# A chunked RWKV inverse kept in PSUM with two pairs in flight, and the one-token sample's state update moved into the feed-forward stage

## The reference, cut to what matters

```python
def step(S, inp):
    r_t, w_t, k_t, v_t, kk_t, b_t = inp
    Sa = jnp.einsum('bhij,bhj->bhi', S, -kk_t)
    S = S * w_t[:, :, None, :] + Sa[..., None] * b_t[:, :, None, :] + v_t[..., None] * k_t[:, :, None, :]
    return S, jnp.einsum('bhij,bhj->bhi', S, r_t)
```

## Time and profile before

| | before |
|---|---|
| median of three runs | 1666.39 us |
| the profiled execution, its span | 1667.1 us |
| TensorE busy | 1566.2 us, 94% of the span |
| VectorE busy | 1140.1 us, 68% |
| ScalarE busy | 858.5 us, 51% |
| GpSimd busy | 262.7 us, 16% |
| layer 0, from the first level product to the last `solve` | 133.46 us (449.41 to 582.87) |
| layer 1, the same stretch | 135.50 us (1268.40 to 1403.90) |

### The profile page before, as it was taken

One profiled execution on the slowest core, in us unless ns is written; L12 is line 12 of the kernel. 1 busy time (PEld: TensorE's weight loads), 2 busy tenths in 40 slices (PEclk: granted clock), 3 DMA queues, 4 the chain that ended last, 5 costly groups with the idle time before them and its releaser, 6 DMA issues. The chain is left out here.

```text
span 1667.1 us, 41414 instructions
## 1 busy us (share of the span) xinstructions
PE 1566.2 (94%) x17379; PEld 1486.8 (89%) x17379; DVE 1140.1 (68%) x1822; ACT 858.5 (51%) x1515; POOL 262.7 (16%) x259
## 2 busy tenths in 40 slices
PE   7999999989799899999999999999997989899997
PEld 6999999987688789999999999989775878799997
DVE  6565587795798667665575656968768886676654
ACT  5444464667444555444354444657673445554443
POOL 0000003001356431000000000030014554300000
PEclk9999999999899999999999999999998999999999
DMA  7555556471244545555454655644703463455552
GB/s 230 178 172 170 168 159 199 130 208 53 59 125 120 144 157 161 194 179 186 143 186 160 194 183 175 189 141 128 215 1 102 126 178 98 131 189 187 183 178 71
DMA packets 280650, 256.28 MB, mean 154 GB/s; under 512 B 48054, under 2 KB 268700, under 8 KB 280450
## 3 DMA queue, kind: packets, MB, share of 16 engines
q1 hardware_dynamic: 276698, 252.05, 48.5%
q10 hardware_dynamic: 3768, 1.59, 0.4%
HBM read 242.22 MB, written 11.38 MB: 152 GB/s over the span
## 5 line engine op out<-in xcount | busy, mean ns | idle before, releaser
L209 ACT ACTIVATE front_hi<-front_raw 128x1024 fp32r<-128x1024 f32 (+2 forms) x230 | 238.5, 1039 | 262.0 <-PE ps L234 255.5
L216 DVE TENSOR_TENSOR front_lo<-front_raw,front_hi 128x1024 fp32r<-128x1024 f32 (+1 forms) x210 | 252.2, 1201 | 109.0 <-ACT front_hi L209 108.2
L209 ACT ACTIVATE out_hi<-out_raw 128x1024 fp32r<-128x1024 f32 (+1 forms) x168 | 173.3, 1038 | 219.1 <-PE ps L234 205.1
L216 DVE TENSOR_TENSOR out_lo<-out_raw,out_hi 128x1024 fp32r<-128x1024 f32 (+1 forms) x148 | 183.9, 1243 | 108.1 <-ACT out_hi L209 107.3
L232 PE MATMUL ps<-front_h_hi,front_hi 128*128 128x264 f32 (+1 forms) x816 | 241.3, 296 | 4.9 <-DVE front_lo L216 3.3
L234 PE MATMUL ps<-front_h_hi,front_lo 128*128 128x264 f32 (+1 forms) x816 | 233.0, 286 | 0.0
L233 PE MATMUL ps<-front_h_lo,front_hi 128*128 128x264 f32 (+1 forms) x816 | 232.7, 285 | 0.0
L232 PE MATMUL ps<-ffn_h_hi,out_hi 128*128 128x264 f32 x704 | 200.7, 285 | 0.1
L233 PE MATMUL ps<-ffn_h_lo,out_hi 128*128 128x264 f32 x704 | 200.0, 284 | 0.0
L234 PE MATMUL ps<-ffn_h_hi,out_lo 128*128 128x264 f32 x704 | 199.8, 284 | 0.0
L232 PE MATMUL ps<-in_h_hi,front_hi 128*128 128x264 f32 x688 | 197.4, 287 | 0.0
(11 more groups left out here) (400 smaller groups left out, 3891.7 us busy)
## 6 DMA issues: line engine op xcount, KB each, us to landing
front_raw<-in_w_in SPq DMA_DIRECT2D x50, 1024.0 KB, 5.2
out_raw<-in_ffn_w_in SPq DMA_DIRECT2D x44, 1024.0 KB, 5.2
front_raw<-in_ffn_w_in SPq DMA_DIRECT2D x40, 1024.0 KB, 5.3
back_sample_rows<-row_scratch SPq DMA_DIRECT2D x160, 128.0 KB, 3.0
out_raw<-in_w_out SPq DMA_DIRECT2D x16, 1024.0 KB, 6.3
front_raw<-in_ffn_w_out SPq DMA_DIRECT2D x16, 896.0 KB, 4.6
out_raw<-in_ffn_w_out SPq DMA_DIRECT2D x16, 896.0 KB, 4.6
front_raw<-in_ffn_w_out SPq DMA_DIRECT2D x8, 1024.0 KB, 5.0
```

Of the source, the lines that this page charges most:

```text
L209: act.activation(self.hi[n % self.RING][:, 0:k, 0:w], self._raw(n), ACT.Copy).then_inc(self.hi_ready, 1)
L216: eng.tensor_tensor(self.lo[n % self.RING][:, 0:k, 0:w], self._raw(n), self.hi[n % self.RING][:, 0:k, 0:w].bitcast(F32), ALU.subtract).the ...
```

## The change

The inverse is made in another way:

- The sum of `x` stays in PSUM: `turn_x` starts it in a bank of its own (`XB + p % 2`), and `level_u` adds its product to it. ACT copies the sum to SBUF after each level (`x_copy(p, i)`).
- The transposed inverse is no longer made by a second product of each level, but by DVE from the copy, as a transposition of 32x32 blocks (`turn_blocks`). Only the last level keeps the product in the transposed form (`finish`).
- Two pairs are in flight: in a round TensorE does levels 2, 3, 4 of pair `g-1` and levels 0, 1 of pair `g`, by turns. `turn_x` of pair `g` stands near the start of its round, `gram` of pair `g+1` near its end, and `mask(g+1)` on DVE behind it.
- In the rounds, a sample pair now has only one product on DVE (old state with two rows, 128x1024) and one sum. The read-out is put together from those sums and from dot products of the vectors (`rec_products`, `rec_sums`, `sample_outputs`). Two rows are loaded, not five.
- The new state is made in the second feed-forward block (`SampleUpdate`): the state and three rows are loaded again, POOL multiplies two rows by a vector, DVE does three operations for each of 8 pairs, at m = 2, 4, 7, 9, 12, 14, 17 and 19 of the 22 steps, and SP stores. These transfers stand in SP's queue between the loads of weight pieces.
- On ACT, `norm3.act_root` moves behind the wait for two stores.

```diff
+class SampleUpdate:
...
+    def sp(self, sp, n):
+        if n == 0:
+            sp.wait_ge(*self.free)
+        if n >= 2:
+            sp.wait_ge(self.done, 3 * (n - 1))
+            sp.dma_start(self.new[n - 2], self.state[(n - 2) % 3][:]).then_inc(self.stored[(n - 2) % 3], 16)
+        if n < RT:
+            for h in range(2):
+                sp.dma_start(self.rows[h * HS:(h + 1) * HS, n % 2].rearrange("p v b j -> p v (b j)"),
...
+            sp.dma_start(self.state[n % 3][:], self.old[n]).then_inc(self.state_in[n % 3], 16)
...
+    def pool(self, pool):
+        for q in range(RT):
+            pool.wait_ge(self.rows_in[q % 2], 32 * (q // 2 + 1))
+            for i, x0 in ((1, self.env.sample_sums[:, q, 0]), (2, self.env.sample_v[:, q])):
+                row = self.rows[:, q % 2, i]
+                pool.tensor_tensor(row, row, x0.unsqueeze(2).to_broadcast([P, NS, HS]), ALU.mult).then_inc(self.products, 1)
...
+    def place(n):
+        return 2 + 5 * n // 2
+
+    def dve(self, dve, m):
...
+        for i, op in ((0, ALU.mult), (1, ALU.add), (2, ALU.add)):
...
+            dve.tensor_tensor(st0[:], st0[:], self.rows[:, q % 2, i], op).then_inc(self.done, 1)
```

```diff
                 for p in range(3, len(pieces)):
                     ws.load(sp, p)
+                    for n in range(RT + 2):
+                        if p == update.place(n) + 10:
+                            update.sp(sp, n)
...
+                def x_copy(p, i):
+                    if i:
+                        act.wait_ge(s("u_ps"), order_of[p, i - 1] + 1)
+                    else:
+                        act.wait_ge(s("x_ps"), p + 1)
+                    act.activation(x[:, p % 2].rearrange("p q t -> p (q t)"), ps[:, XB + p % 2, 0:4 * C], ACT.Copy).then_inc(s("x_in"), 1)
...
+                def turn_blocks(p, i):
+                    flat = lambda a: a.rearrange("p q t -> p (q t)")
+                    dve.wait_ge(s("x_in"), copied[p, i])
+                    dve.transpose(flat(xt[:, p % 3]), flat(x[:, p % 2])).then_inc(s("xt_in"), 1)
...
+                def sample_products(m):
...
+                    dve.tensor_tensor(prod[:], state[:, m % 2].unsqueeze(1).to_broadcast([P, 2, NS, HS]), rows[:, m % 2],
+                                      ALU.mult).then_inc(s("sampled"), 1)
+
+                def sample_sums(m):
+                    dve.wait_ge(s("sampled"), m + 1)
+                    dve.tensor_reduce(sums[:, m], prod[:], AX.X, ALU.add).then_inc(s("summed"), 1)
...
                 def level_u(p, i):
-                    n = LV * p + i
+                    n = order_of[p, i]
                     pe.wait_ge(s("t1_in"), n + 1)
-                    if n:
-                        pe.wait_ge(s("xt_up"), n)
-                    if i < LV - 1:
-                        blocks(UB, xt[:, p % 3], t1[:]).then_inc(s("u_ps"), 1)
-                    blocks(UB + 1, t1[:], xt[:, p % 3]).then_inc(s("ut_ps"), 1)
+                    if i:
+                        pe.wait_ge(s("xt_in"), turned_blocks(p, i))
+                    if i < LV - 1:
+                        blocks(XB + p % 2, 0, xt[:, p % 3], t1[:, n % 2], False, i == LV - 2).then_inc(s("u_ps"), 1)
+                    else:
+                        blocks(XB + p % 2, 4 * C, t1[:, n % 2], xt[:, p % 3]).then_inc(s("u_ps"), 1)
...
                 def solve(p):
 
-                    pe.wait_ge(s("xt_up"), LV * (p + 1))
+                    pe.wait_ge(s("xt_up"), p + 1)
```

More of the change, by code:

```diff
@@ L333, in act_hi @@
     def act_hi(self, act, k):
+        if k == 0 and self.update is not None:
+            self.update.wait_stored(act)
         act.wait_ge(self.x_ready, k + 1)
@@ L403, in pool @@
                 self.ws.split_lo(pool, n)
+        if self.update is not None:
+            self.update.pool(pool)
     def act(self, act):
@@ L474, in dve @@
                 self.side.dve(dve)
+            if self.update is not None:
+                self.update.dve(dve, m)
         hidden_lo(FT - 1)
@@ L1920, in _ @@
                         short_split_hi(1)
-                    if 0 <= l < RT:
-                        t1_copy(l, 2)
+                    if 0 <= b < RT:
+                        t1_copy(b, 3)
+                    if g < RT:
+                        tokens(g, 1)
+                    if p >= 0:
+                        square(p)
+                    if 0 <= b < RT:
+                        x_copy(b, 4)
                     if g == RT - 1:
@@ L2108, in _ @@
                     if g < RT:
-                        start(g)
+                        turn_blocks(g, 2)
                     if g < 4:
```

437 lines of the change are left out of this document (230 added, 207 removed).

## The result

The changed kernel takes **1684.71 us** (median of 4 runs, 1680.36 to 1687.53) against 1668.1 us for the kernel before (1666.23 to 1671.9; the three runs named above and a fourth). The ratio is **1.0099 [1.0076, 1.0123]**: slower by about 16.6 us, where 1652 was predicted, with 1636 to 1667 as the range. The profiled execution has a span of 1681.3 us against 1667.1, so it holds 14.2 of the loss.

What follows compares the result with a forecast made beforehand. TensorE, busy for 94% of the span, was taken to bound the kernel: 1667.1 - 15.3 for the rounds + 1.0 for the feed-forward blocks = 1652.8, put at 1652 us for the median, range 1636 to 1667.

Steps and rivals of the forecast that it cites:

- The work removed: Second product of levels 0 to 3 goes: 64 groups at 0.51 us, 32.6 us of TensorE in all.
- The start: First rounds of a layer: levels with nothing beside them and late masks put round 2 6.9 us behind.
- The steady round: Rounds 3 to 6: 15.86 us less 4 groups at 0.51 is 13.8, if the idle time stays.
- the signs given for a wrong prediction: Steady round above 15 us, round 8 as long as before, or TensorE waiting for `out_lo` or `inner` beside update rows.
- The feed-forward block: Second feed-forward block, which gets the state update: 0.5 us more a layer, 1.0 in all.
- The transfer term: Feed-forward block: 10.5 MB more a layer, 90 GB/s on top of 179, fits, as round 7 moved 268.
- the lump: Feed-forward block: three VectorE update operations together, 2.1 to 3.7 us, hidden by a 5.95 us step and weights loaded ahead.
- The sign given for it: Feed-forward block: TensorE waiting for `out_lo` or `inner` beside the update rows would show the prediction wrong.
- the rival with a chance of 0.08: Feed-forward block: update lumps reach TensorE or weights queue too long; 16 lumps at 2 us cost 32: 1684; chance 0.08.
- ACT's order sets the round: Rounds 3 to 8 each wait 1.2 us more for ACT's fixed list of copies: 1666 to 1667; chance 0.19.
- More comes back: Steady round falls to about 12.8 us and the late start is half as late: 17 us more, 1636; chance 0.22.
- the chain through the masks: `gram`, masks, POOL, `start`, `turn_x` across rounds bound; round stays near 15.5 us, 1667 or more; chance 0.05.

Runs made afterwards that it cites:

- timed_by_layer: `early_start` with VectorE's update split, layer 0 loads as in `late_burst`, layer 1 loads in three spread pieces, output weights one piece a round: 1653.4 us.
- early_start: Changed kernel with VectorE's first rounds reordered: bonus work ahead of the transpositions, five short-branch operations moved from round 1 to rounds 2 to 6: 1672.1 us.
- late_burst: `early_start` with VectorE's update split into three places, and a round's 768 KB of loads issued about 1 us later, behind VectorE's transfer: 1662.2 us.

## Why the prediction was wrong, by its own steps

- **The work removed**: right. The second product has 256 records; TensorE has 1020 records fewer. Its busy time fell by 13.1 us only; how much of the rest is the lower clock and how much the overlap of records was not taken apart. VectorE is busy for 65.7 us of the rounds of layer 0; "near 65 of 125" was said. The transposition took 0.45 us, 0.42 was taken.

```profile
L2272 PE MATMUL ps<-back_inverse_t,back_n_x x256: 213/218/218, 469.5 to 1410.1; 64*64 64x64 f32 x128
```

- **The start**: right in size for what it counted. The first solve came 7.2 us later; 6.9 was the sum. What it lacked is the clock, 0.64 over the 4 us that followed in layer 0. And 4.9 us of the loss were avoidable: the reason the step gives, work on other heads behind `turn_blocks`, was a matter of order.
- **The steady round**: the mechanism was right, "15.86 us less 4 groups at 0.51 is 13.8, if the idle time stays". The seven intervals between solves were predicted as 104.0 us in sum. In layer 1 of `timed_by_layer` they are 13.8, 14.1, 14.7, 14.0, 14.7, 15.0 and 18.2, 104.5. In the changed kernel they were 116.3 in layer 0 and 108.4 in layer 1. **This is the first step that failed**: "if the idle time stays". It did not, because the change also packed the loads of a round, eleven pieces before, into one burst, and I read the transfers by their sum alone ("with fewer transfers beside the three weight pieces"). The runs that leave the loads out or move them show that the bursts stop TensorE, by their moment against the instruction fetches. The largest single miss is round 6 of layer 0, 19.5 us where 13.8 was predicted: the order of SP's queue in the changed kernel starts the weights in that round, while the prediction had them in round 7. What such a burst does could be read in the rows: the old kernel's round of 18.20 us had 14.31 of TensorE beside a DMA share of 0.96, with one stop of 2.9 us in it, and I booked the difference as idle time that would shrink to 15.3. Of the signs given for a wrong prediction this one came: rounds 4 and 5 of layer 0 were above 15. Round 8 did get shorter, 18.5 us in layer 0 where 17.5 was predicted.
- **The feed-forward block**: **the second step that failed**. "I put 0.5 us a layer" measured 4.2 and 6.2. The transfer term was checked against bandwidth ("268 GB/s were moved in round 7, so there is room") and the lump against the weights' lead ("weight blocks lie up to four ahead"). The first was misread: 90 on top of 179 GB/s is 269, and the row it leans on has 268 GB/s at a DMA share of 0.96, so it shows that the queue would be full, not that there was room. Either cost is small alone, 2.3 and 2.0 us over both layers. But the second check used a cover that the first had used up: 242 GB/s were moved at a share of 0.92, a weight piece landed after 8.2 us instead of 5.2, the lead was gone, and lumps of 2.3 to 3.1 us, inside the 2.1 to 3.7 predicted, then reached TensorE. The sign given for it came too: TensorE waited for `inner` beside the update rows.
- **The rivals**: the time is that of the rival with a chance of 0.08, 1684, yet its mechanism gave 10.4 us of the loss and not 32, so that the time fits is luck. "ACT's order sets the round" did not come: TensorE waited 3.2 us for the copies in layer 0 of the changed kernel. "More comes back" did not either; the best rounds are at 13.8. Nor does the chain through the masks bound the round: TensorE waited for `start` and `finish` mainly in rounds 1 and 2 (3.6 and 2.6 us), and the best rounds hold the same chain.

In sum: predicted -15.3 for the rounds, measured +3.6; predicted +1.0 for the blocks, measured +10.4. -14.3 against +14.0.

## What to carry to other kernels

If two edits each lean on the same slack, price them together: a transfer that makes weights land later uses up the lead behind which a lump of VectorE was to hide, so ask what covers each when the other is there, and cut new work on a shared engine into pieces shorter than the shortest cover. Read the room for transfers from the DMA share of a row and not from its GB/s, and read transfers not only by bytes: when a rewrite packs small loads into one burst, look at the instruction queue and at stops with "issue" as the releaser, and try the burst at another moment before believing in a slow loop. When an order is rewritten, put work that nobody awaits into the gaps of its first rounds.

## What the hardware showed beyond that

- TensorE's instructions come in packets of 16 KB (0.05 MB for 3), three in a round of some 375 products with their weight loads. Rounds in which one met a burst of 768 KB had stops of up to 1.8 us, those with the burst of the output weights stops of 0.8 to 3.7 us. Bursts 1 us later took the stops at one product from one layer and enlarged them in the other. That a fetch waits behind the packets of a data queue fits this; the trace shows the times, not the waiting.
- A standstill of 1.7 to 2.6 us was in some executions followed by a granted clock of 0.54 to 0.64 over the next 2.5 to 4 us, and in others not: 1.00 followed on the 1.71 us of `early_start`, on 2.55 us ahead of the first solve of the changed kernel's layer 1, on 2.83 us in `late_burst`. Where the clock falls, a stop costs more than its length: of two rounds with a stop of 1.71 us, one took 17.62 us with TensorE busy for 15.23, the other 16.07 with 13.63. What decides between them stays open.
- The Trainium skill, "SBUF — State Buffer", on the shared port pair, was cited for VectorE's operations stretching beside GpSimd's. This trace agrees. Of the 24 operations of layer 0, the four that lie beside a GpSimd product took 1.53 us, 0.98 of it beside the product, and the 20 others 0.68 to 0.70:

```profile
L600 DVE TENSOR_TENSOR upd_state<-upd_state,upd_rows x24: 682/693/1529, 671.9 to 777.7; 128x512 f32<-128x512 f32 x24
```
